# One small step per token group in a two-layer encoder kernel: three groups of narrow fp32 matmuls, placed side by side in TensorE's rows, are put into one place each and issued one kind after the other

## The chip, the cores and the metric

The kernel runs on one core of a Trainium2 chip. The metric is the device time in microseconds (us) of one execution. The time of a kernel is the median of several executions; the profiler also recorded one execution of the kernel before, and all rows of the trace come from that one.

## The reference

Two sequences (512 and 2048 tokens, 1024 wide) go through two layers. Each layer has one input projection, three groups of heads (RWKV-7 time mixing, latent attention, gMLP) and one output projection. The change touches only the preparation of the RWKV-7 branch (6 heads of 64 channels, 384 channels in all):

```python
kk = l2_normalize(heads(k * k_k))             # each head's 64 channels divided by their norm
def direction(d, lw, la, reverse):            # d = 0 forward, 1 backward
    w = jnp.exp(-DECAY_SCALE * jax.nn.sigmoid(decay_w0[d] + jnp.tanh(lw) @ decay_up[d]))
    a = jax.nn.sigmoid(iclr_a0[d] + la @ iclr_up[d])
    k_rep = k * (1 + (a - 1) * k_a)
    return wkv7_scan(heads(r), heads(w), kk, heads(a) * kk, heads(k_rep), heads(v), reverse)
```

`lw` and `la` have 64 columns for each direction, and `decay_up`, `iclr_up` are 64 x 384.

## The kernel before

All data are fp32, channels on the partitions. Each layer runs as a row of stages, with a barrier of all engines between two of them: `feature_projection`, `token_projection` (the one that is changed), `rwkv_scan`, `mla_attention`, `out_projection`.

`token_projection` does two things at once. TensorE computes the part of the input projection that is wanted token by token: 20 tiles of 128 tokens, three pieces each (512, 512 and 480 columns), 60 pieces (`project(n)`), each piece eight matmuls over the contraction; they use four of the eight PSUM banks, and ScalarE copies each piece out (`empty(n)`, L704). Between the pieces TensorE does the small products of the RWKV preparation for groups of 512 tokens, five groups (`g`), ten pieces beside each. The orders of TensorE, ScalarE, VectorE and SyncE are written out by hand, engine by engine. One fp32 matmul is two matmul instructions in the trace, each with its own weight load; the text calls such an instruction a pass.

The small products of a group, in TensorE's order, with `BA = 3` blocks `m` of 128 channels (two heads):

- `norm` (L851): the sums of squares of each head. Three matmuls accumulate into one bank. The constant matrix has `NR = 70` columns, so the six sums land three times, on partitions 0 to 5, 32 to 37 and 64 to 69. ScalarE takes the root of these 70 partitions (L760), VectorE bounds them from below and takes the reciprocal (L976, L978).
- `w` of direction 0 (L822, `lora`): three matmuls, contraction over 64 partitions.
- `bonus` (L863): three matmuls.
- piece n+1, then `inv` (L869): the six reciprocals are spread over the 128 channels of each block, by three matmuls with a contraction of 6. Block `m` reads partitions 32m to 32m+5, so the three stand in three different row groups of the array. VectorE multiplies `kk` with them (L988).
- `a` of direction 0 and `w` of direction 1 (L822): block by block in turn, a0, w0, a1, w1, a2, w2. Direction 0 reads partitions 0 to 63, direction 1 partitions 64 to 127. ScalarE takes the sigmoids in the same order (L710).
- pieces n+2, n+3, then `a` of direction 1 (L822, three matmuls), piece n+4, the block products (`blocks`, L839), pieces n+5 to n+9. The block products of direction 1 come after piece n+10 and before the next group's `norm`.

The small products share the other four banks in turn, in the order in which `uses.add` lists them; a product whose bank was used four places before waits until ScalarE or VectorE has emptied that one (`bank_free`). Around the change the places are: bonus 0, 1, 2, inv 0, 1, 2, then the six of `a` and `w`. VectorE's `direction(g, 0)` begins when the last `a` is through its sigmoid (L919), ScalarE's `blend` (L742) when L919 is done, and VectorE's `decay_sums(g, 1)` when the last `w` is.

Of the kernel before, what the change touches and what calls it, by code (L numbers as in the profile page):

```python
# [24 lines left out]
ACT = mybir.ActivationFunctionType  # L25
AX = mybir.AxisListType

P = 128
# [4 lines left out]
G = 512  # L33
# [4 lines left out]
HA, DH = 6, 64  # L38
BA = HA * DH // P
CH = 64  # L40
# [15 lines left out]
R_ADAB, R_QKW, R_LNW, R_LNB, R_ALL = np.cumsum([0, 3 * D, 2 * DQK, CW, CW]).tolist()  # L56

K_ID, K_BD, K_MA, K_KX, K_LV, K_RST, K_HS, K_HT, K_ALL = np.cumsum(
    [0, 128, 128, 512, 4 * CH, CH, 512, BA * (32 * (BA - 1) + HA), P]).tolist()


def slot_of(kind, parity):
# [431 lines left out]
def token_projection(l, wt, wt_in, nc, d, ps, kc, col, amod, eps, ident):  # L494
# [4 lines left out]
    HALF = (slice(0, CH), slice(CH, P))  # L499
    NP = 2 * BA * (G // SUB)  # L500
    PER = 10
    NR = 32 * (BA - 1) + HA
    pieces = [(n, c, min(c + 512, WT)) for n in range(NT) for c in range(0, WT, 512)]
    PT = len(pieces) // NT

# [3 lines left out]
    uses = Uses(4, 4)  # L509
# [5 lines left out]
    for g in range(NG):  # L515
        if g:
            add_blocks(g - 1, 1)
        for m in range(2):
            uses.add(("norm", g, m), "act")
        for m in range(BA):  # L520
            uses.add(("w", g, 0, m), "act")
        for m in range(BA):
            uses.add(("bonus", g, m), "dve")
        for m in range(BA):
            uses.add(("inv", g, m), "dve")
        for m in range(BA):
            uses.add(("a", g, 0, m), "act")
            uses.add(("w", g, 1, m), "act")
        for m in range(BA):
            uses.add(("a", g, 1, m), "act")  # L530
        add_blocks(g, 0)
    add_blocks(NG - 1, 1)

    with ExitStack() as ctx:
        def sb(name, shape):
            return ctx.enter_context(nc.sbuf_tensor(f"prep{l}_" + name, shape, F32))
# [5 lines left out]
        low = sb("low", [P, 2, G])  # L542
        ga = sb("ga", [P, BA, G])
        dup = sb("dup", [P, 2, BA * P])
        km = sb("km", [P, BA])
        norm = sb("norm", [NR, G])
        rkb = sb("rkb", [P, BA, P])
        kk = sb("kk", [P, BA, G])
        tmp = sb("tmp", [P, BA, G])
# [11 lines left out]
        with stage(nc, "up h_in0 h_in1 h_in2 rk_in0 rk_in1 val_in low_in ga_in z_filled z_out piece_sent0 piece_sent1 piece_sent2 "  # L561
# [136 lines left out]
            def _(a):  # L698
# [4 lines left out]
                    a.wait_ge(z_filled, n + 1)  # L703
                    a.activation(st[:, n % NB, 0:c1 - c0], ps[:, tiles.bank(pieces[n]), 0:c1 - c0], ACT.Copy).then_inc(z_out, 1)  # L704

                def sigmoid(kind, g, e, m):
                    out, c = {"w": (sg, C_W0), "a": (aa, C_A0)}[kind]
                    u = (kind, g, e, m)
                    a.wait_ge(filled, uses.ready(u))
                    a.activation(out[:, m, :], ps[:, uses.bank(u), :], ACT.Sigmoid, bias=col[:, c + e * BA + m:c + e * BA + m + 1]).then_inc(act_out, 1)  # L710

                def powers(g, e):
                    a.wait_ge(decayed, 2 * g + e + 1)
# [31 lines left out]
                for g in range(NG):  # L745
                    n = PER * g
                    a.wait_ge(rk_arrived[g % 2], 16 * (g // 2 + 1))
                    if g:
                        a.wait_ge(scaled_out, 2 * g)
                    for b in range(BA):  # L750
                        a.activation(kk[:, b, :], rk_in[g % 2][:, BA + b, :], ACT.Copy, scale=col[:, C_KK + b:C_KK + b + 1]).then_inc(keys, 1)
                    a.wait_ge(keys, BA * (g + 1))
                    a.activation(tmp[:, :, :], kk[:, :, :], ACT.Square).then_inc(squares, 1)
                    a.wait_ge(low_in, 16 * (g + 1))
                    a.activation(low[:, 0, :], low[:, 0, :], ACT.Tanh).then_inc(lora_in, 1)
                    empty(n)
                    if g:
                        blocks_out(g - 1, 1)
                    a.wait_ge(filled, uses.ready(("norm", g, 1)))
                    a.activation(norm[:, :], ps[0:NR, uses.bank(("norm", g, 0)), :], ACT.Sqrt).then_inc(act_out, 2)  # L760
                    for m in range(BA):
                        sigmoid("w", g, 0, m)
                    powers(g, 0)
                    a.wait_ge(filled, uses.ready(("bonus", g, BA - 1)))
                    for m in range(BA):
                        sigmoid("a", g, 0, m)
                        sigmoid("w", g, 1, m)
                    blend(g, 0)
                    empty(n + 1)
                    a.wait_ge(ga_in, 16 * (g + 1))  # L770
                    a.activation(ga[:, :, :], ga[:, :, :], ACT.Silu).then_inc(silu, 1)
                    empty(n + 2)
                    a.wait_ge(bonus_out, g + 1)
                    for m in range(BA):
                        last = a.activation(ga[:, m, :], ga[:, m, :], ACT.Copy, scale=col[:, C_GNW + m:C_GNW + m + 1])
                    last.then_inc(gated, 1)
                    empty(n + 3)
                    powers(g, 1)
                    a.wait_ge(scaled_out, 2 * g + 1)
                    for m in range(BA):  # L780
                        sigmoid("a", g, 1, m)
                    empty(n + 4)
                    blocks_out(g, 0)
                    empty(n + 5)
                    empty(n + 6)
                    if g:
                        turn(g - 1)
                    blend(g, 1)
                    empty(n + 7)
                    empty(n + 8)  # L790
                    empty(n + 9)
# [8 lines left out]
            def _(pe):  # L800
# [12 lines left out]
                def bank_free(u):  # L813
                    f = uses.former(u)
                    if f:
                        pe.wait_ge(act_out if f[0] == "act" else dve_out, f[1])
                    return ps[:, uses.bank(u), :]

                def lora(kind, g, e, m):
                    n = "wa".index(kind)  # L820
                    b = bank_free((kind, g, e, m))
                    pe.matmul(b, dup[DH * e:DH * e + DH, n, m * P:(m + 1) * P], low[DH * e:DH * e + DH, n, :], start=True, stop=True).then_inc(filled, 1)  # L822

                def blocks(g, e):
                    pe.wait_ge(scaled_out, 2 * g + e + 1)
# [16 lines left out]
                for g in range(NG):  # L842
                    n = PER * g
                    project(n)
                    if g:
                        blocks(g - 1, 1)
                    pe.wait_ge(squares, g + 1)
                    bank_free(("norm", g, 1))
                    b = bank_free(("norm", g, 0))
                    for m in range(BA):  # L850
                        last = pe.matmul(b[0:NR, :], kc[:, K_HS + m * NR:K_HS + (m + 1) * NR], tmp[:, m, :], start=(m == 0), stop=(m == BA - 1))  # L851
                    last.then_inc(filled, 2)
                    pe.wait_ge(lora_in, g + 1)
                    if g == 0:
                        pe.wait_ge(up, 32)
                    for m in range(BA):
                        lora("w", g, 0, m)
                    pe.wait_ge(rk, g + 1)
                    if g == 0:
                        pe.wait_ge(ready, 1 + BA)  # L860
                    for m in range(BA):
                        u = ("bonus", g, m)
                        pe.matmul(bank_free(u), rkb[:, m, :], aa[:, m, :], start=True, stop=True).then_inc(filled, 1)  # L863
                    project(n + 1)
                    pe.wait_ge(norms, g + 1)
                    for m in range(BA):
                        u = ("inv", g, m)
                        b = bank_free(u)
                        pe.matmul(b, kc[32 * m:32 * m + HA, K_HT:K_HT + P], norm[32 * m:32 * m + HA, :], start=True, stop=True).then_inc(filled, 1)  # L869
                    for m in range(BA):  # L870
                        lora("a", g, 0, m)
                        lora("w", g, 1, m)
                    project(n + 2)
                    project(n + 3)
                    for m in range(BA):
                        lora("a", g, 1, m)
                    project(n + 4)
                    blocks(g, 0)
                    project(n + 5)
                    project(n + 6)  # L880
                    project(n + 7)
                    project(n + 8)
                    project(n + 9)
# [1257 lines left out]
def shape_constants():  # L2141

    a, b = np.arange(P)[:, None], np.arange(P)[None, :]
    chunk = a // CH == b // CH
    k = np.zeros((P, K_ALL), np.float32)
# [13 lines left out]
    k[:, K_RST:K_RST + G] = np.arange(G) % CH != 0  # L2159
    for m in range(BA):  # L2160
        for h in range(HA):
            for n in range(BA):
                k[:, K_HS + m * (32 * (BA - 1) + HA) + 32 * n + h] = 2 * m + np.arange(P) // DH == h
            k[32 * m + h, K_HT:K_HT + P] = 2 * m + np.arange(P) // DH == h
    freqs = np.float32(10000.0) ** (-np.arange(16, dtype=np.float32) / np.float32(16))
    pos = np.concatenate([np.arange(T0), np.arange(T1)]).astype(np.float32)
    ang = (pos[:, None] * freqs[None, :]).astype(np.float32)
# [52 lines left out]
```

## Time and profile before

| | |
|---|---|
| median of 3 runs | 5484.08 us (5480.12 to 5485.88) |
| the profiled execution | 5480.12 us, span of its instructions 5478.1 us |
| busy: TensorE, weight loads, VectorE, ScalarE, GpSimd | 95%, 51%, 52%, 38%, 12% |
| mean granted TensorE clock | 0.983 |

A row of the timeline has the start and the length of a merged run of like instructions in us, the engine, the line of the kernel, the operation, what it writes and reads, the shapes, and the count; in brackets stands the idle time of the engine before it and what ended it. PE is TensorE's matmul side, PEld its weight loads, DVE VectorE, ACT ScalarE. A matmul's own length is modelled and overlaps the next one's, so the time that a run takes on TensorE is read from its start to the start of the next run.

### The profile page before, as it was taken

What the parts mean: (1) busy time and instruction counts of PE and PEld (TensorE: products, weight loads), DVE (VectorE), ACT (ScalarE), POOL (GpSimd) and SP (SyncE); (2) the same over time, 40 slices, a digit from 0 to 9 for tenths busy, and PEclk for the clock granted to TensorE, in tenths of its full rate; (3) what the DMA queues carried; (4) which work ended last, traced back from release to release, by engine and by line L of the source; (5) the groups of instructions that cost most, each with busy time, mean ns of one, the idle gap of its engine ahead of it and who ended that gap; (6) DMA issues with size and microseconds to landing.
All of it is one profiled execution on the core that took longest, in us unless ns stands there. A gap on an engine that the chain in (4) does not pass through costs nothing. (4 is left out here: it accounts for less than half of the span.)

```text
span 5478.1 us, 94771 instructions
## 1 busy us (share of the span) xinstructions
PE 5208.6 (95%) x38844; PEld 2808.7 (51%) x38844; DVE 2834.5 (52%) x4438; ACT 2068.8 (38%) x3470; POOL 641.6 (12%) x1110
## 2 busy tenths in 40 slices
PE   8999999899979999989989999998999799999899
PEld 3444444488854444444444444444788544444454
DVE  2221487555545555556522214875555555555565
ACT  1211556255544444421112115562455444444211
POOL 0000000044520000001100000000445200000011
PEclk9999999999999999999999999999999999999999
DMA  5311566565650111036343115664656501110353
GB/s 225 139 67 56 191 218 201 157 161 145 162 139 11 36 28 25 6 111 222 118 162 139 69 55 194 216 202 153 162 145 164 137 14 35 25 25 6 106 173 118
DMA packets 570089, 646.04 MB, mean 118 GB/s; under 512 B 228336, under 2 KB 455152, under 8 KB 559872
## 3 DMA queue, kind: packets, MB, share of 16 engines
q1 hardware_dynamic: 569072, 638.88, 37.3%
q8 instruction: 313, 5.13, 0.4%
q14 instruction: 112, 0.92, 0.1%
q10 hardware_dynamic: 592, 1.11, 0.1%
HBM read 372.74 MB, written 267.13 MB: 117 GB/s over the span
## 5 line engine op out<-in xcount | busy, mean ns | idle before, releaser
L490 PE MATMUL ps<-feat_hT,w_features 128*128 128x512 f32 x2240 | 972.5, 592 | 0.0
L810 PE MATMUL ps<-w_tokens,prep_hT 128*128 128x512 f32 (+1 forms) x1920 | 821.2, 587 | 23.1 <-DMA prep_hT<-s_ht 23.1
L1706 PE MATMUL ps<-att_K,att_Q 96*128 96x512 f32 x1632 | 744.3, 599 | 31.5 <-DMA att_K<-s_qkt 21.8
L490 PEld LDWEIGHTS ps<-feat_hT,w_features 128*128 128x128 f32 x2240 | 420.4, 190 | 505.9 <-issue 503.2
L1820 DVE TENSOR_REDUCE att_mx<-ps 128x1 f32<-128x1024 f32 x384 | 470.3, 1225 | 286.0 <-PE ps L1706 286.0
L810 PEld LDWEIGHTS ps<-w_tokens,prep_hT 128*128 128x128 f32 x1920 | 363.4, 191 | 469.5 <-issue 440.9
L1713 PEld LDWEIGHTS ps<-kc,att_pr 128*128 128x128 f32 x3264 | 362.8, 141 | 433.0 <-issue 319.1
L2101 PE MATMUL ps<-w_out,fin_yT 128*128 128x512 f32 x1280 | 569.0, 598 | 2.5 <-DVE fin_yT L2051 2.5
L1784 ACT ACTIVATE att_PT<-ps 128x512 f32<-128x512 f32 x384 | 228.1, 594 | 691.1 <-PE ps L1713 690.9
L1713 PE MATMUL ps<-kc,att_pr 128*128 128x128 f32 x3264 | 479.2, 279 | 5.3 <-DVE att_PT L1829 2.5
L1706 PEld LDWEIGHTS ps<-att_K,att_Q 96*128 96x128 f32 x1632 | 296.9, 192 | 334.0 <-issue 256.9
L1775 ACT ACTIVATE att_pr<-ps,att_nb 128x1024 f32<-128x1024 f32 x384 | 428.3, 1115 | 80.1 <-DVE att_nb L1822 80.0
L1829 DVE COPY att_PT<-ps 128x512 f32<-128x512 f32 x384 | 265.2, 691 | 322.0 <-PE ps L1713 322.0
L1729 PE MATMUL ps<-att_PT,att_V 128*64 128x512 f32 x1536 | 411.2, 617 | 0.3
L2101 PEld LDWEIGHTS ps<-w_out,fin_yT 128*128 128x128 f32 x1280 | 238.9, 192 | 274.8 <-issue 271.6
L380 ACT ACTIVATE feat_z<-ps 128x512 f32<-128x512 f32 x110 | 65.8, 598 | 603.8 <-PE ps L490 603.8
L1979 POOL TENSOR_SCALAR fin_rv<-fin_st 128x1 f32<-128x1 f32 x40 | 17.7, 442 | 2035.9 <-DVE fin_st L1997 2035.9
L419 DVE SCALAR_TENSOR_TENSOR feat_co<-feat_z,col,feat_co 128x512 f32<-128x512 f32 (+1 forms) x88 | 66.1, 751 | 300.1 <-ACT feat_co L352 300.1
L404 DVE TENSOR_SCALAR feat_hT<-ps,amod 128x512 f32<-128x512 f32 x80 | 63.8, 809 | 283.8 <-PE ps L477 283.6
L1421 DVE TENSOR_TENSOR scan_tok<-ps,scan_u 64x384 f32<-64x384 f32 x160 | 88.8, 555 | 218.1 <-PE ps L1542 190.2
L1252 POOL TENSOR_SCALAR scan_ss<-scan_ss 128x2 f32<-128x2 f32 x40 | 18.2, 455 | 1434.8 <-ACT scan_csq L1295 1434.8
L704 ACT ACTIVATE prep_st<-ps 128x512 f32<-128x512 f32 (+1 forms) x120 | 69.1, 583 | 268.1 <-PE ps L810 268.1
(226 smaller groups left out, 6735.8 us busy)
## 6 DMA issues: line engine op xcount, KB each, us to landing
s_sc<-prep_sc SPq DMA_DIRECT2D x20, 3072.0 KB, 9.0
scan_src<-s_sc SPq DMA_DIRECT2D x160, 384.0 KB, 4.9
s_qkt<-scan_qT SPq DMA_DIRECT2D x40, 576.0 KB, 4.2
fin_z<-s_zt SPq DMA_DIRECT2D x40, 576.0 KB, 5.1
s_zf<-feat_co SPq DMA_DIRECT2D x88, 256.0 KB, 2.6
s_ht<-feat_hT SPq DMA_DIRECT2D x10, 2048.0 KB, 7.9
prep_hT<-s_ht SPq DMA_DIRECT2D x40, 512.0 KB, 5.8
s_zt<-prep_st SPq DMA_DIRECT2D x80, 256.0 KB, 3.5
```

The costliest lines, as they stand in the source:

```text
L490: last = pe.matmul(b, wf[:, k, i * P:(i + 1) * P], hT[g % 2][:, k, :], start=(k == 0), stop=(k == KD - 1))
L704: a.activation(st[:, n % NB, 0:c1 - c0], ps[:, tiles.bank(pieces[n]), 0:c1 - c0], ACT.Copy).then_inc(z_out, 1)
L810: last = pe.matmul(ps[:, tiles.bank(pieces[n]), 0:c1 - c0], hT[j % NH][:, k, :], wt[:, k, c0:c1], start=(k == 0), stop=(k == KD - 1))
L1421: last = v.tensor_tensor(out_, pair(u, BA * CH)[HALF[p], :, :].rearrange("p o (m i) -> p o m i", m=BA), u0[HALF[p], s, :, :].rearrange("p ...
L1706: pe.matmul(ps[:, c, :], Q[:, t * P:(t + 1) * P], K[:, k0:k0 + G], start=True, stop=True).then_inc(scored, 1)
L1713: last = pe.transpose(ps[:, BANK_T + x % 2, k * P:(k + 1) * P], pr[:, n % 2, (TPG * x + k) * P:(TPG * x + k + 1) * P], ident)
L1729: last = pe.matmul(ps[DV * half:DV * half + DV, BANK_O, :], V[:, kb + (TPG if k else 0), 0:DV], PT[:, kb, :], start=(i == 0), stop=final_p ...
L1775: a.activation(pr[:, n % 2, 2 * half * G:2 * (half + 1) * G], ps[:, 2 * half:2 * half + 2, :].rearrange("p b n -> p (b n)"), ACT.Exp, bias ...
L1784: a.activation(evict_target(n, x), bank(BANK_T), ACT.Copy).then_inc(act_t, 1)
L1820: ch.link(v.tensor_reduce(mx[:, n % 2, half:half + 1], ps[:, 2 * half:2 * half + 2, :].rearrange("p b n -> p (b n)"), AX.X, ALU.max))
L1829: v.tensor_copy(evict_target(n, x), bank(BANK_T + 1)).then_inc(dve_t, 1)
L2101: last = pe.matmul(b, yT[n % TPG][:, k, :], wo[:, k, G * c:G * (c + 1)], start=(k == 0), stop=(k == KD - 1))
```

## The change

Three things are changed. The constant for the norms has 6 columns instead of 70, so that the six sums exist once, on partitions 0 to 5. The three `inv` matmuls all read these partitions, with three different 6 x 128 constants beside one another. And the six products of `a` (direction 0) and `w` (direction 1) are issued as a0, a1, a2, w0, w1, w2, with their banks and ScalarE's sigmoids in the same order. The constants' tile grows by 64 columns.

```diff
 K_ID, ..., K_HS, K_HT, K_ALL = np.cumsum(
-    [0, 128, 128, 512, 4 * CH, CH, 512, BA * (32 * (BA - 1) + HA), P]).tolist()
+    [0, 128, 128, 512, 4 * CH, CH, 512, BA * HA, BA * P]).tolist()
...
         for m in range(BA):
             uses.add(("a", g, 0, m), "act")
+        for m in range(BA):
             uses.add(("w", g, 1, m), "act")
...
-        norm = sb("norm", [NR, G])
+        norm = sb("norm", [HA, G])
...
-                    a.activation(norm[:, :], ps[0:NR, uses.bank(("norm", g, 0)), :], ACT.Sqrt).then_inc(act_out, 2)
+                    a.activation(norm[:, :], ps[0:HA, uses.bank(("norm", g, 0)), :], ACT.Sqrt).then_inc(act_out, 2)
...
-                    for m in range(BA):
-                        sigmoid("a", g, 0, m)
-                        sigmoid("w", g, 1, m)
+                    sigmoids("a", g, 0)
+                    sigmoids("w", g, 1)
...
-                        last = pe.matmul(b[0:NR, :], kc[:, K_HS + m * NR:K_HS + (m + 1) * NR], tmp[:, m, :], start=(m == 0), stop=(m == BA - 1))
+                        last = pe.matmul(b[0:HA, :], kc[:, K_HS + m * HA:K_HS + (m + 1) * HA], tmp[:, m, :], start=(m == 0), stop=(m == BA - 1))
...
                     for m in range(BA):
                         u = ("inv", g, m)
-                        b = bank_free(u)
-                        pe.matmul(b, kc[32 * m:32 * m + HA, K_HT:K_HT + P], norm[32 * m:32 * m + HA, :], start=True, stop=True).then_inc(filled, 1)
-                    for m in range(BA):
-                        lora("a", g, 0, m)
-                        lora("w", g, 1, m)
+                        pe.matmul(bank_free(u), kc[0:HA, K_HT + m * P:K_HT + (m + 1) * P], norm[:, :], start=True, stop=True).then_inc(filled, 1)
+                    lora("a", g, 0)
+                    lora("w", g, 1)
```

`lora` and `sigmoids` now hold the loop over the three blocks themselves; for `w` of direction 0 and `a` of direction 1 that is the order of before.

## Rows read from the trace of the kernel before

**Rows 1.** The page: span and the engines' busy time.

```profile
span 5478.1 us, 94771 instructions
PE 5208.6 (95%) x38844; PEld 2808.7 (51%) x38844; DVE 2834.5 (52%) x4438; ACT 2068.8 (38%) x3470; POOL 641.6 (12%) x1110
```

**Rows 2.** Windows, changed stage of layer 0: stretch, length, busy PE, PEld, DVE, ACT, POOL, clock.

```profile
552.00:1004.00 452.00, 444.44 (x1881) 195.56 (x1882) 319.97 (x462) 248.59 (x321) 0.00 (x0) 1.00 0.60 199
```

**Rows 3.** Timeline of the changed place in the first group.

```profile
576.90 1.13 PE L869 MATMUL ps<-prep_norm,kc 6*128 6x512 f32 x6
577.96 4.94 PE L822 MATMUL ps<-prep_low,prep_dup 64*128 64x512 f32 x12
578.05 1.89 DVE L988 TENSOR_TENSOR prep_kk<-ps,prep_kk 128x512 f32<-128x512 f32 x3 [3.04 <-PE ps L869]
578.80 0.29 PEld L822 LDWEIGHTS ps<-prep_low,prep_dup 64*128 64x128 f32 x2 [0.54 <-DVE prep_kk L988]
579.16 1.28 ACT L710 ACT_TABLE_LOAD   x1 [1.26 <-PE ps L822]
579.40 0.29 PEld L822 LDWEIGHTS ps<-prep_low,prep_dup 64*128 64x128 f32 x2 [0.30 <-DVE prep_kk L988]
...
580.46 0.69 ACT L710 ACTIVATE prep_aa<-ps,col 128x512 f32<-128x512 f32 x1
581.05 0.68 ACT L710 ACTIVATE prep_sg<-ps,col 128x512 f32<-128x512 f32 x1
581.20 0.29 PEld L822 LDWEIGHTS ps<-prep_low,prep_dup 64*128 64x128 f32 x2 [0.91 <-ACT prep_aa L710]
...
582.83 1.48 PE L810 MATMUL ps<-w_tokens,prep_hT 128*128 128x480 f32 x3
583.57 1.76 DVE L919 TENSOR_TENSOR prep_tmp<-prep_aa,prep_kk 128x1536 f32<-128x1536 f32 x1 [3.63 <-ACT prep_aa L710]
```

**Rows 4.** Timeline of PE at the same place in the last group of layer 1.

```profile
3674.20 1.13 PE L869 MATMUL ps<-prep_norm,kc 6*128 6x512 f32 x6
3675.27 4.94 PE L822 MATMUL ps<-prep_low,prep_dup 64*128 64x512 f32 x12
3680.14 1.12 PE L810 MATMUL ps<-w_tokens,prep_hT 128*128 128x512 f32 x2
```

**Rows 5.** Timeline of PE, then of its weight loads, at the products of one direction alone.

```profile
596.34 2.84 PE L822 MATMUL ps<-prep_low,prep_dup 64*128 64x512 f32 x6
599.11 1.12 PE L810 MATMUL ps<-w_tokens,prep_hT 128*128 128x512 f32 x2
596.34 0.29 PEld L822 LDWEIGHTS ps<-prep_low,prep_dup 64*128 64x128 f32 x2 [0.76 <-issue]
596.87 0.19 PEld L822 LDWEIGHTS ps<-prep_low,prep_dup 64*128 64x128 f32 x1 [0.24 <-issue]
597.30 0.19 PEld L822 LDWEIGHTS ps<-prep_low,prep_dup 64*128 64x128 f32 x1 [0.24 <-issue]
```

**Rows 6.** Timeline of PE before a two-column product in a later stage.

```profile
2692.42 1.02 PE L2101 MATMUL ps<-w_out,fin_yT 128*128 128x512 f32 x2
2693.37 0.60 PE L161 MATMUL ps<-fin_ada,sg 128*2 128x512 f32 x2
```

**Rows 7.** Timeline from the block products of one group to the next norms.

```profile
648.27 1.63 PE L839 MATMUL ps<-prep_sc 64*64 64x64 f32 x96
649.27 3.95 ACT L729 ACTIVATE prep_lst<-ps 32x384 f32<-32x384 f32 x8 [0.23 <-PE ps L839]
651.38 2.76 PE L851 MATMUL ps<-prep_tmp,kc 128*70 128x512 f32 x6 [1.48 <-ACT prep_lst L729]
```

**Rows 8.** What PE waited for at L851 in the whole span: us, times.

```profile
ACT prep_lst L729: 12.2, 8
```

**Rows 9.** Timeline of VectorE and PE before the second block products of a group.

```profile
731.26 1.83 DVE L898 TENSOR_TENSOR prep_sc<-prep_aa,prep_ip 128x768 f32<-128x768 f32 x2
737.90 1.63 PE L839 MATMUL ps<-prep_sc 64*64 64x64 f32 x96
```

More of the change, by code:

```diff
@@ L501, in token_projection @@
     PER = 10
-    NR = 32 * (BA - 1) + HA
     pieces = [(n, c, min(c + 512, WT)) for n in range(NT) for c in range(0, WT, 512)]
@@ L704, in empty, with sigmoids @@
                     a.activation(st[:, n % NB, 0:c1 - c0], ps[:, tiles.bank(pieces[n]), 0:c1 - c0], ACT.Copy).then_inc(z_out, 1)
-                def sigmoid(kind, g, e, m):
+                def sigmoids(kind, g, e):
                     out, c = {"w": (sg, C_W0), "a": (aa, C_A0)}[kind]
-                    u = (kind, g, e, m)
-                    a.wait_ge(filled, uses.ready(u))
-                    a.activation(out[:, m, :], ps[:, uses.bank(u), :], ACT.Sigmoid, bias=col[:, c + e * BA + m:c + e * BA + m + 1]).then_inc(act_out, 1)
+                    for m in range(BA):
+                        u = (kind, g, e, m)
+                        a.wait_ge(filled, uses.ready(u))
+                        a.activation(out[:, m, :], ps[:, uses.bank(u), :], ACT.Sigmoid, bias=col[:, c + e * BA + m:c + e * BA + m + 1]).then_inc(act_out, 1)
                 def powers(g, e):
@@ L759, in _ @@
                     a.wait_ge(filled, uses.ready(("norm", g, 1)))
-                    a.activation(norm[:, :], ps[0:NR, uses.bank(("norm", g, 0)), :], ACT.Sqrt).then_inc(act_out, 2)
-                    for m in range(BA):
-                        sigmoid("w", g, 0, m)
+                    a.activation(norm[:, :], ps[0:HA, uses.bank(("norm", g, 0)), :], ACT.Sqrt).then_inc(act_out, 2)
+                    sigmoids("w", g, 0)
                     powers(g, 0)
                     a.wait_ge(filled, uses.ready(("bonus", g, BA - 1)))
-                    for m in range(BA):
-                        sigmoid("a", g, 0, m)
-                        sigmoid("w", g, 1, m)
+                    sigmoids("a", g, 0)
+                    sigmoids("w", g, 1)
                     blend(g, 0)
@@ L779, in _ @@
                     a.wait_ge(scaled_out, 2 * g + 1)
-                    for m in range(BA):
-                        sigmoid("a", g, 1, m)
+                    sigmoids("a", g, 1)
                     empty(n + 4)
@@ L817, in bank_free, with lora @@
                     return ps[:, uses.bank(u), :]
-                def lora(kind, g, e, m):
+                def lora(kind, g, e):
                     n = "wa".index(kind)
-                    b = bank_free((kind, g, e, m))
-                    pe.matmul(b, dup[DH * e:DH * e + DH, n, m * P:(m + 1) * P], low[DH * e:DH * e + DH, n, :], start=True, stop=True).then_inc(filled, 1)
+                    for m in range(BA):
+                        b = bank_free((kind, g, e, m))
+                        pe.matmul(b, dup[DH * e:DH * e + DH, n, m * P:(m + 1) * P], low[DH * e:DH * e + DH, n, :], start=True, stop=True).then_inc(filled, 1)
                 def blocks(g, e):
@@ L855, in _ @@
                         pe.wait_ge(up, 32)
-                    for m in range(BA):
-                        lora("w", g, 0, m)
+                    lora("w", g, 0)
                     pe.wait_ge(rk, g + 1)
@@ L867, in _ @@
                         u = ("inv", g, m)
-                        b = bank_free(u)
-                        pe.matmul(b, kc[32 * m:32 * m + HA, K_HT:K_HT + P], norm[32 * m:32 * m + HA, :], start=True, stop=True).then_inc(filled, 1)
-                    for m in range(BA):
-                        lora("a", g, 0, m)
-                        lora("w", g, 1, m)
+                        pe.matmul(bank_free(u), kc[0:HA, K_HT + m * P:K_HT + (m + 1) * P], norm[:, :], start=True, stop=True).then_inc(filled, 1)
+                    lora("a", g, 0)
+                    lora("w", g, 1)
                     project(n + 2)
                     project(n + 3)
-                    for m in range(BA):
-                        lora("a", g, 1, m)
+                    lora("a", g, 1)
                     project(n + 4)
@@ L2161, in shape_constants @@
         for h in range(HA):
-            for n in range(BA):
-                k[:, K_HS + m * (32 * (BA - 1) + HA) + 32 * n + h] = 2 * m + np.arange(P) // DH == h
-            k[32 * m + h, K_HT:K_HT + P] = 2 * m + np.arange(P) // DH == h
+            k[:, K_HS + m * HA + h] = 2 * m + np.arange(P) // DH == h
+            k[h, K_HT + m * P:K_HT + (m + 1) * P] = 2 * m + np.arange(P) // DH == h
     freqs = np.float32(10000.0) ** (-np.arange(16, dtype=np.float32) / np.float32(16))
```

## The prediction

> **What bounds the kernel now.** I read the page first: TensorE is busy for 95% of the span, every other engine for about half or less [rows 1]. The windows of the changed stage say the same of the place itself: of 452 us TensorE is busy for 444, at the full granted clock (1.00, the level of 2.4 GHz), VectorE for 320, ScalarE for 249 [rows 2]. So the stage is as long as TensorE's list of passes, and the question is what the change does to that list, then whether a wait of TensorE swallows or adds something. Then I read the timeline at the place. The three `inv` matmuls, six passes, take from 576.90 to 577.96, 1.06 us, and the six products of `a` and `w`, twelve passes, from 577.96 to 582.83, 4.87 us: 5.93 together [rows 3]. In the last group of layer 1 it is 1.07 and 4.87 again, 5.94 [rows 4]. The ten places (five groups, two layers) agree to a hundredth of a us, so I work out one and multiply by ten.
>
> **The price of one pass.** Where three matmuls of the same shape as `a` and `w` stand in one row group (direction 1 alone), the first pass starts at 596.34, the next at 596.87, then 597.30: 0.53, and from then on 0.43 a pass [rows 5]. The 0.10 over is the weight load that nothing covers on the first pass. From the last pass to the next piece it is 0.52 (596.34 + 0.53 + 4 x 0.43 = 598.59, next start 599.11). Six serial passes so take 2.77 us, entry and exit included [rows 5]. The six `inv` passes of before take 1.06, that is two passes' time and the exit [rows 3]: the three row groups do run at once. That is the whole gain of the old layout there.
>
> **Part 1: `inv` in one row group.** Six passes one behind the other cost what the six of rows 5 cost, 2.77 instead of 1.06: +1.71 us a group. The trace has no run of matmuls with a contraction of 6 in one row group, so the bounds are: 2.77 as in rows 5, and, if every pass pays 0.53 as a first one does, 5 x 0.53 + 0.52 = 3.17, +0.40. I take 2.77, because only the number of partitions differs and the time of a pass is that of its 512 columns in both. Below 2.77 I see nothing, since the partitions are the same ones.
>
> **Part 2: a0, a1, a2, w0, w1, w2.** The old order alternates between partitions 0 to 63 and 64 to 127, so passes can overlap; w0 starts at 578.80 and a1 at 579.40, 0.60 later where two serial passes take 0.96 [rows 3]. But it hardly uses that, because it runs into its banks: w0 waits for VectorE to empty the bank of inv 0 (first load at 578.80), a1 and w1 for the next two, a2 for ScalarE's first sigmoid (581.20, idle 0.91) and w2 for the second [rows 3]. It gets 4.87, where twelve serial passes with entry and exit are 0.53 + 10 x 0.43 + 0.52 = 5.35. Now the new order, in us from the first `inv` pass:
> - The `a` passes begin at 2.77: a0 at 2.77 and 3.30, a1 at 3.73 and 4.16, a2 at 4.59 and 5.02. Their banks: a0 follows bonus 2, a1 follows inv 0, a2 inv 1, w0 inv 2. VectorE takes 0.69 for each and began 1.15 after the first pass (578.05), that is 0.62 after that block's second pass [rows 3]; now it begins at 1.15, 2.01 and 2.87 and the banks are free, 0.74 later, at 1.9, 2.8 and 3.6. None of them is waited for any more.
> - w0 reads the other half, so its first pass starts with a2's last one, at 5.02, the second at 5.55, through at 5.98.
> - w1 needs the bank of a0. ScalarE's table load began 0.67 after a0's second pass began (578.49 to 579.16), the sigmoid 1.30 later, it took 0.69, and TensorE went on 0.05 after [rows 3]. Now: 3.30 + 0.67 + 1.30 + 0.69 + 0.05 = 6.01. w1 starts at 6.01 with its load uncovered, 6.53, and w2 (its bank, a1's, is free at 6.6) at 6.96 and 7.39; the next piece starts 0.52 later, at 7.91.
> So the `a` and `w` part takes 7.91 - 2.77 = 5.14 instead of 4.87: +0.27. If w0 did not overlap a2's last pass, it would be the serial 5.35, +0.48; if neither overlap nor waits cost anything more than they do here, it cannot be under 5.35 - 0.43 = 4.92, +0.05.
>
> **Part 3: the norms with 6 columns.** The number of passes stays six. ScalarE's root and VectorE's bound and reciprocal have 512 elements on each partition as before, so their lengths stay. What may change is the entry: a product with few columns behind a full one starts 0.95 after the last but one full pass began (2692.42 to 2693.37), where two passes are 0.86 [rows 6], so such a change costs 0.09. In eight of the ten groups the norms stand behind the block products and a wait of about 1.5 for ScalarE [rows 7, 8], which covers it, and the weight load there, no longer 70 columns wide, may be some hundredths shorter. That leaves 0.09 in the first group of each layer, 0.2 us in all, and perhaps as much back: I take nothing, with bounds of -0.5 and +2.0 (a full 0.20 of entry and uncovered load in all ten groups). The 64 more columns of constants are 32 KB at the start, behind the first transposes' wait, which other work ends; nothing.
>
> **What the other engines do with it.** The last `a` is through its sigmoid 0.57 later than now (a2's sigmoid is the third in ScalarE's row instead of the fifth, but the row starts 1.71 later), so L919 starts about 0.6 later and everything behind it on VectorE too, while TensorE's next piece starts 1.98 later. VectorE's last operation before the block products ended at 733.09, and they began at 737.90 [rows 9]: this slack of 4.8 grows. ScalarE's last `w` sigmoid comes some 1.7 later, but `blend` waits for L919 anyway. `low` is read no longer than before as seen from TensorE's later products, and SyncE's queue has nothing new. So nothing gets late, and nothing that TensorE waits for gets earlier in a way that it would feel.
>
> **Sum.** 1.71 + 0.27 = 1.98 us a group, ten groups: +19.8 us. The profiled execution took 5480.12 us (2.0 of it outside the span of 5478.1), so it would be 5499.9. The median of the runs is 5484.08, 3.96 above that execution; on it I get 5503.9.
>
> **Rivals.**
> - *TensorE's wait swallows it.* In eight groups TensorE waits before the norms for ScalarE's copies L729, 12.2 us in all [rows 8]. Were those copies held by something that does not move with TensorE, the wait would shrink by the delay: 19.8 - 12.2 = +7.6, 5491.7, within 0.2%. It decides from 8.8 us swallowed (1.1 of the 1.5 in each). Against it: L729 starts 1.0 after the block products began and was itself waiting for them (idle 0.23, released by PE) [rows 7], so the wait moves along whole. This is the one way that ends at "not slower".
> - *`inv` pays its loads.* With 0.53 for each pass, 0.40 more a group: +23.8, 5507.9.
> - *Every pass in one row group pays its load.* Five more in `inv` and ten or so in `a` and `w`, 15 x 0.10 = 1.5 a group: +35, 5519. Rows 5 speak against it: the loads of passes three and four follow at 0.43 in the same row group. By the Trainium skill (TensorE: Matmul & The Clock Gate, in "Part 3: Packing small matmuls — row/col tiling") a weight load overlaps a running matmul only where the row group differs; by that the sum would be this one, by the row it is mine. The trace disagrees with the rule, at 0.43 a pass.
> - *No overlap of w0 with a2:* +0.21 a group, 5506.0.
>
> **How the numbers follow.** The forecast has 0.78, no overlap 0.07, `inv` paying its loads 0.06, every pass paying 0.02, the swallowed delay 0.04, and 0.03 is left for something faster that I can't name from the rows. Runs of one kernel spread by 5.8 us here, so 0.2% (11 us) is what can be told from no change. The range runs from 5496 (the forecast less its bounds of 2.2 for part 2 and 0.5 for part 3, and the spread) to 5511 (`inv` with its loads, and the spread). Slower by over 0.2% then has 0.93, within it 0.04, faster 0.03.
>
> **What would show it.** In the profile after: L869's six passes from start to the next run's start 2.77 (3.17 if loads are paid); the `a` and `w` run 5.14, with one wait of TensorE for the first sigmoid and none for VectorE's L988; L919 starting 7.24 after the first `inv` pass instead of 6.67; the wait before the norms still 1.5; busy time of TensorE higher by about 20 us, and the slack before the second block products above 6. The prediction is wrong if the `inv` passes in one row group still take about 1.1, or if the ten groups lengthen by another amount than the place itself does.

## The result, and the profile of the changed kernel

The changed kernel takes 5519.53 us (median of four runs, 5514.96 to 5524.57), the kernel before 5484.26. The ratio is 1.0065, 95% interval 1.0048 to 1.0083: 0.65% slower. I had forecast slower, by 19.8 us; it is 35.3, and 5519.5 lies above the range that I gave (5496 to 5511). The profiled execution is not one of the four and was longer than all of them: 5531.59 us, span 5529.7.

The page of the kernel after, against [rows 1]: TensorE 45.3 us more of busy time and 18.5 more of weight loads, the other engines as before, the number of instructions the same.

```profile
span 5529.7 us, 94771 instructions
PE 5253.9 (95%) x38844; PEld 2827.2 (51%) x38844; DVE 2836.4 (51%) x4438; ACT 2069.1 (37%) x3470; POOL 641.7 (12%) x1110
```

The timeline of PE at the changed place, in the first and third group of layer 0 and in the last of layer 1, where [rows 3, 4] have 5.93 and 5.94 us from the first `inv` pass to the next piece:

```profile
577.85 2.84 PE L866 MATMUL ps<-prep_norm,kc 6*128 6x512 f32 x6
580.61 5.78 PE L821 MATMUL ps<-prep_low,prep_dup 64*128 64x512 f32 x12
586.33 1.88 PE L808 MATMUL ps<-w_tokens,prep_hT 128*128 128x480 f32 x4
...
762.58 2.84 PE L866 MATMUL ps<-prep_norm,kc 6*128 6x512 f32 x6
765.35 7.87 PE L821 MATMUL ps<-prep_low,prep_dup 64*128 64x512 f32 x12
773.15 1.22 PE L808 MATMUL ps<-w_tokens,prep_hT 128*128 128x512 f32 x1
...
3717.67 2.84 PE L866 MATMUL ps<-prep_norm,kc 6*128 6x512 f32 x6
3720.44 5.78 PE L821 MATMUL ps<-prep_low,prep_dup 64*128 64x512 f32 x12
3726.15 1.12 PE L808 MATMUL ps<-w_tokens,prep_hT 128*128 128x512 f32 x2
```

The `inv` passes take what I said, 2.77 (577.85 to 580.61, 762.58 to 765.35; 2.96 and 2.99 in two of the ten groups). The passes of `a` and `w` do not: 5.72, 7.80, 5.71 instead of 5.14. And the ten places are no longer alike, which is the first hint that it is not a matter of the instruction list. The windows of two of these `inv` and `a`/`w` stretches show what it is (stretch, length, busy PE, PEld, DVE, ACT, POOL, then the granted clock):

```profile
577.84:580.61 2.77, 2.77 (x7) 1.03 (x6) 1.38 (x2) 1.00 (x1) 0.00 (x0) 1.00 0.00 0
580.61:586.32 5.71, 5.71 (x13) 2.56 (x12) 1.04 (x2) 3.68 (x5) 0.00 (x0) 0.70 0.00 0
762.58:765.35 2.77, 2.77 (x7) 1.03 (x7) 1.38 (x2) 1.00 (x1) 0.00 (x0) 1.00 0.00 0
765.35:773.15 7.80, 7.80 (x14) 3.06 (x13) 2.28 (x2) 4.39 (x6) 0.00 (x0) 0.51 0.01 2
```

TensorE is busy without a gap through the `inv` passes, at a granted clock of 1.00, and in the stretch behind them it runs at 0.70 and 0.51: part or nearly all of it at the lower of its two levels, 1.2 GHz instead of 2.4. In the two groups with 2.96 and 2.99 the clock falls before the last `inv` pass is through (0.93 and 0.92 over those passes). The same windows at all ten places have a clock of 0.50 to 0.70 and a mean length of 6.76 us where I had 5.14:

```profile
sum 67.62, PE 67.62 PEld 28.44 DVE 16.86 ACT 40.81 POOL 0.00; mean PE 6.76 PEld 2.84 DVE 1.69 ACT 4.08 POOL 0.00
```

The whole stage of layer 0 was at 1.00 before [rows 2]; now, over the same work:

```profile
553.00:1026.00 473.00, 466.12 (x1881) 204.06 (x1882) 320.88 (x462) 249.58 (x321) 0.00 (x0) 0.96 0.59 195
```

From TensorE's first piece to the last group's second block products the stage of layer 0 takes 476.6 us (553.27 to 1029.89) where it took 455.3 (552.48 to 1007.80), and that of layer 1 475.8 where it took 455.0: +42.1 in both, 19.8 of passes and 22.3 more. Of the 22.3 some 16.6 lie in the ten places themselves (5.7 at the least, 7.9 at the most for `a` and `w`), the rest in the pieces behind. The other 9.5 us by which the profiled execution's span grew lie outside the changed stage; 7.1 of them between its last block products and the first attention passes, where `rwkv_scan` stands (599.6 and 600.8 us in the two layers, where it was 596.8 and 596.4).

### The profile page after: what moved, and what is told of

Same layout as the page of the kernel before. It is cut to its first block and busy times, and to the rows that moved or that the text cites. A ratio compares the mean times of both kernels' runs of the same rounds, so it can differ in the third digit from the quotient of the medians.

```text
span 5529.7 us, 94771 instructions
## 1 busy us (share of the span) xinstructions
PE 5253.9 (95%) x38844; PEld 2827.2 (51%) x38844; DVE 2836.4 (51%) x4438; ACT 2069.1 (37%) x3470; POOL 641.7 (12%) x1110
## 5 line engine op out<-in xcount | busy, mean ns | idle before, releaser
L808 PEld LDWEIGHTS ps<-w_tokens,prep_hT 128*128 128x128 f32 x1920 | 365.8, 192 | 475.8 <-issue 450.2
```

Of the source, the lines that this page charges most:

```text
L808: last = pe.matmul(ps[:, tiles.bank(pieces[n]), 0:c1 - c0], hT[j % NH][:, k, :], wt[:, k, c0:c1], start=(k == 0), stop=(k == KD - 1))
```

## Experiments

To compare the runs I read one more view of each: the granted clock over the 12 us from the first `inv` pass, at the ten places. "Falls" below is the number of places where it is under 1.00. The kernel before has 0, the changed one 10. The count comes from one profiled execution of each kernel. Each time is a median, with the ratio to runs of the kernel before on the same chip and its 95% interval; the ratio can differ by up to 0.06% from the quotient of the two medians, and where a text below gives microseconds, they are the difference of the medians.

| run | what differs | us (before) | ratio (interval) | falls |
|---|---|---|---|---|
| e1_inv_only | alternating a, w; serial inv | 5505.32 (5478.42) | 1.0054 (1.0040 to 1.0067) | 9 |
| e2_order_only | grouped a, w; inv as before | 5487.73 (5478.42) | 1.0014 (1.0005 to 1.0024) | 1 |
| e3_inv_full_rows | changed, inv over 128 partitions | 5494.73 (5478.42) | 1.0034 (1.0022 to 1.0047) | 0 |
| e4_piece_between | changed, a piece behind inv | 5580.24 (5478.42) | 1.0187 (1.0173 to 1.0201) | 10 |
| e5_inv_32_rows | changed, inv over 32 partitions | 5509.95 (5482.71) | 1.0052 (1.0033 to 1.0071) | 6 |
| e6_inv_64_rows | changed, inv over 64 partitions | 5495.97 (5482.71) | 1.0024 (1.0012 to 1.0035) | 0 |
| e7_norm_70_columns | changed, norms 70 columns | 5520.50 (5482.71) | 1.0067 (1.0050 to 1.0084) | 10 |
| e8_three_times_side_by_side | before, inv three times over | 5517.64 (5482.71) | 1.0065 (1.0050 to 1.0080) | 10 |
| e9_two_row_groups | changed, inv in two row groups | 5509.80 (5482.30) | 1.0056 (1.0043 to 1.0070) | 7 |
| e10_tables_early | before, ScalarE tables early | 5469.17 (5482.30) | 0.9972 (0.9963 to 0.9982) | 0 |
| e11_changed_again | the changed kernel | 5518.75 (5482.30) | 1.0068 (1.0054 to 1.0082) | 10 |

### One part at a time: e1_inv_only and e2_order_only

```diff
# e1_inv_only, against the kernel after
-                    lora("a", g, 0)
-                    lora("w", g, 1)
+                    for m in range(BA):
+                        lora("a", g, 0, [m])
+                        lora("w", g, 1, [m])
...
# e2_order_only, against the kernel before
                     for m in range(BA):
                         lora("a", g, 0, m)
+                    for m in range(BA):
                         lora("w", g, 1, m)
```

In both the banks and the sigmoids follow the same order.

> The changed kernel with the six products of a and w put back in the alternating order a0, w0, a1, w1, a2, w2; the norms with 6 columns and the three inv products in one row group stay. Theory 1 (the six serial inv passes, which use 6 rows, make the granted clock of TensorE fall; the grouped order of a and w only adds its +0.27 a group): the clock shows stretches at half in most of the ten groups as in the changed kernel, and the time is +17 us of passes plus 10 to 30 us of lost clock over the kernel before, 5511 to 5530. Rival 2 (the grouped order, 5.1 us of passes in one half of the rows behind the inv passes, is needed for the fall): no half-clock stretches in the groups, 5501.

> The kernel before with one part of the change: a0, a1, a2, w0, w1, w2 in banks, on TensorE and on ScalarE; the inv products stay in three row groups and the norms keep 70 columns. Theory 1: about +0.3 us a group, 5487, no half-clock stretch in the groups. Rival 2: half-clock stretches appear in the groups, 5497 or more.

The serial `inv` passes alone bring the falls (9 of 10) and 26.9 of the microseconds. The one place without a fall shows the bare price in TensorE's timeline:

```profile
3703.43 2.84 PE L866 MATMUL ps<-prep_norm,kc 6*128 6x512 f32 x6
3706.20 1.99 PE L821 MATMUL ps<-prep_low,prep_dup 64*128 64x512 f32 x8
3709.43 1.70 PE L821 MATMUL ps<-prep_low,prep_dup 64*128 64x512 f32 x4 [1.25 <-ACT prep_aa L710]
3711.06 1.12 PE L808 MATMUL ps<-w_tokens,prep_hT 128*128 128x512 f32 x2
```

That is 7.64 us, 1.70 more than before, all of it `inv`. The 26.9 is the low end of the 27 to 47 expected over the kernel before. The grouped order alone costs 9.3 us by the medians (interval 3 to 13); its place takes 6.21 us in nine of ten groups (before 5.94, so +0.27, as summed), 2.7 us in all. The tenth had a fall behind `inv` passes of only 1.06 us:

```profile
3405.27 1.13 PE L871 MATMUL ps<-prep_norm,kc 6*128 6x512 f32 x6
3406.34 7.46 PE L824 MATMUL ps<-prep_low,prep_dup 64*128 64x512 f32 x12
```

So the order adds a little of each, and serial `inv` passes are not the only thing that a fall can stand behind. How many falls there are seems to change from run to run: of the eleven runs of e2 the shortest, 5474.05 us, has a mean clock of 0.984 and the longest, 5496.92, one of 0.980. But the grouped order is not needed for the falls (e1 has nine without it), and rival 2 is out.

### Are six-row passes the cause: e3_inv_full_rows, e6_inv_64_rows, e5_inv_32_rows

```diff
-        norm = sb("norm", [HA, G])
+        norm = sb("norm", [P, G])
...
-                        pe.matmul(bank_free(u), kc[0:HA, K_HT + m * P:K_HT + (m + 1) * P], norm[:, :], start=True, stop=True).then_inc(filled, 1)
+                        pe.matmul(bank_free(u), kc[:, K_HT + m * P:K_HT + (m + 1) * P], norm[:, :], start=True, stop=True).then_inc(filled, 1)
...
+                v.memset(norm[:, :], 0.0).then_inc(ready, 1)
```

(e5 and e6: 32 and 64 in place of P. The added rows hold zeros on both sides, so the sums stay.)

> The changed kernel, but each inv product contracts over all 128 partitions: the tile of reciprocals has 128 partitions with zeros in 122 of them, and the constants are zero there too. The number of serial passes and their columns stay. Theory 1 in the form that the few rows in use matter: the clock stays at full level in the groups, and the time is the +1.98 a group of my sum or a little less (no change of row group before inv), 5500 to 5504. If only that the passes are serial, or that their products are mostly nothing, matters: as the changed kernel, 5515 to 5530.

> As e3_inv_full_rows, but with a contraction over 64 partitions (58 of them zero). The products of a and w, and those of w and a alone elsewhere in the group, use 64 rows and the clock does not fall at them in the kernel before. If rows decide: few falls or none, and +17 to +25. If falls come as in the changed kernel, zeros or the run of 7.9 us without a pass over all rows matter.

> As e3_inv_full_rows, but the inv products contract over 32 partitions (26 of them zero) instead of 128. If the clock goes by the number of rows of the array that the serial passes use, and 32 are still few: falls at most of the ten places, as in the changed kernel, +27 to +41 over the kernel before. If 6 rows were the special case: no falls, +16 to +20.

The passes are as many and as serial as in the changed kernel, the numbers that they multiply are zeros where they were nothing, and the falls are gone at 128 and 64 partitions, while 32 partitions had 6. The times follow: +16.3, +13.3, +27.2; the first two are 3 to 4 us less than expected. The timeline of e3 has the place at full clock:

```profile
580.78 2.74 PE L866 MATMUL ps<-prep_norm,kc 128*128 128x512 f32 x6
583.45 2.84 PE L821 MATMUL ps<-prep_low,prep_dup 64*128 64x512 f32 x8
586.69 1.98 PE L821 MATMUL ps<-prep_low,prep_dup 64*128 64x512 f32 x4 [0.40 <-ACT prep_aa L711]
588.60 1.88 PE L808 MATMUL ps<-w_tokens,prep_hT 128*128 128x480 f32 x4
```

`inv` 2.67, `a` and `w` 5.15, together 7.82; my sum had 2.77 and 5.14. The 0.10 that `inv` is short of tells what the entry is paid for: here `inv` contracts over as many partitions as the piece before it, and its first load (580.36) runs beside that piece's last pass. In e6 it is the first `a` that follows passes with as many partitions as its own, 64, and there `a` and `w` take 5.04. So where TensorE has no wait before a run, the 0.10 of entry goes with a change in the number of rows. In e5 a place without a fall shows the sum itself, 763.02 to 770.93, 7.91:

```profile
763.02 2.84 PE L866 MATMUL ps<-prep_norm,kc 32*128 32x512 f32 x6
765.79 2.84 PE L821 MATMUL ps<-prep_low,prep_dup 64*128 64x512 f32 x8
769.02 1.98 PE L821 MATMUL ps<-prep_low,prep_dup 64*128 64x512 f32 x4 [0.40 <-ACT prep_aa L711]
770.93 1.55 PE L808 MATMUL ps<-w_tokens,prep_hT 128*128 128x512 f32 x3
```

### One row group, or few rows for long: e8_three_times_side_by_side and e9_two_row_groups

```diff
# e8_three_times_side_by_side, against the kernel before
-                        pe.matmul(b, kc[32 * m:32 * m + HA, K_HT:K_HT + P], norm[32 * m:32 * m + HA, :], start=True, stop=True).then_inc(filled, 1)
+                    for r in range(3):
+                        for m in range(BA):
+                            b = ps[:, uses.bank(("inv", g, m)), :]
+                            last = pe.matmul(b, kc[32 * m:32 * m + HA, K_HT:K_HT + P], norm[32 * m:32 * m + HA, :], start=True, stop=True)
+                            if r == 2:
+                                last.then_inc(filled, 1)
...
# e9_two_row_groups, against the kernel after: AT = (0, 32, 0), the sums on partitions 0 to 5 and 32 to 37
+                        pe.matmul(bank_free(u), kc[AT[m]:AT[m] + HA, K_HT + m * P:K_HT + (m + 1) * P], norm[AT[m]:AT[m] + HA, :], start=True, stop=True).then_inc(filled, 1)
```

> The kernel before with its three inv products issued three times over (the first two results are overwritten by the same values), in their three row groups: 18 passes that take about 1.06 + 2 x 0.86 = 2.8 us, as long as the six serial ones of the changed kernel, with three row groups at work instead of one. VectorE's first product comes 1.7 later, all three banks at once, so a and w run 4.87 as before: +1.7 a group, +17. If the rows at work decide: no falls, +17. If it is the length of a stretch of products with a contraction of 6: falls at most places, +27 or more.

> The changed kernel with the sums on partitions 0 to 5 and 32 to 37: inv 0 and inv 2 read the first copy, inv 1 the second, so that two of the three products overlap and the inv passes take about 1.06 + 0.86 = 1.9 us instead of 2.77. If the length of the stretch of 6-row passes makes the clock fall, 1.9 us lies between the 1.06 that never had a fall and the 2.8 that had one at nearly every place: falls at some of the ten places, +12 to +25. If any serial 6-row product does it: falls at most places, +25 or more. If only a stretch as long as 2.8 does: none, +12.

e8 is the surprise: three row groups at work, falls at all ten places. The windows of its `inv` stretch (18 passes in 2.78 us), of the `a` and `w` stretch behind it and of the 12 us from its start:

```profile
578.93:581.71 2.78, 2.78 (x19) 1.10 (x19) 0.00 (x0) 1.01 (x1) 0.00 (x0) 1.00 0.00 0
581.71:586.94 5.23, 5.23 (x15) 2.69 (x12) 1.89 (x3) 3.65 (x6) 0.00 (x0) 0.67 0.00 0
578.93:590.93 12.00, 12.00 (x41) 5.80 (x41) 5.14 (x6) 7.33 (x11) 0.00 (x0) 0.86 0.01 1
```

So being placed in one row group is not what lowers the clock; three times six rows side by side for 2.8 us do it as well, and for 1.06 us, as in the kernel before, they don't. In e9 the `inv` passes take 1.91 us, in between, and 7 of 10 places fall.

The time of e8 can't be taken for the price of its falls, though it is nearly that of the changed kernel. All ten places have 0.86 over their 12 us, 0.14 x 12 = 1.7 us of clock each, and the fall lies within the `a` and `w` stretch (0.33 x 5.23 = 1.7). But that stretch takes 5.2 to 5.3 us where it took 4.87, so most of the 1.7 costs nothing there; TensorE had idle loads of 0.91 and 0.28 us in this stretch before, waiting for ScalarE, which may be what hides it. The changed stage grew by 10.7 and 11.2 us in the two layers (467.7 and 467.9 us from the first piece to the end of the last block products, where it was 457.0 and 456.7): 2.2 a group, 1.72 of it passes. The profiled execution's span grew by 38.9, and the other 17.0 lie outside the changed stage, most of them where `rwkv_scan` of layer 0 stands. The kernel before first, then e8:

```profile
1009.43:1606.22 596.79, 532.46 (x11701) 432.00 (x11700) 315.59 (x488) 276.34 (x477) 242.95 (x342) 0.97 0.54 143
1022.12:1630.46 608.34, 541.12 (x11701) 438.90 (x11701) 315.31 (x488) 276.51 (x477) 242.69 (x342) 0.96 0.53 140
```

Why the clock is lower there too, in a stage that no edit touched, stays open.

### Apart from a and w: e4_piece_between

```diff
+                    project(n + 2)
                     lora("a", g, 0)
                     lora("w", g, 1)
-                    project(n + 2)
                     project(n + 3)
```

> The changed kernel with piece n+2 (sixteen full passes, some 7 us) moved between the inv products and those of a and w. If the six inv passes alone make the clock fall: half-clock stretches stay, now in the piece, 5512 or more. If it takes the inv passes and the grouped passes of half the rows in one row (8 us without a full pass): no half-clock stretches in the groups, and the sum of before holds, 5504 to 5506.

Falls at all ten places, now in the piece: the `inv` passes suffice, with full passes behind them too. But the time, +101.8, is no measure of that, as the edit makes `a` late on ScalarE and VectorE. What e4 waits for at the block products (L838), over the whole span:

```profile
PE ps L838 <- ACT prep_aa L711: 39.8, 12, 4.1
```

These waits were none before. They stand at the first block products of each group, 3.7 to 4.1 us each (and two of 0.2), not at the second ones of [rows 9], whose slack holds. In the first group:

```profile
604.69 7.13 PE L808 MATMUL ps<-w_tokens,prep_hT 128*128 128x512 f32 x16
614.68 1.84 ACT L711 ACTIVATE prep_aa<-ps,col 128x512 f32<-128x512 f32 x3
615.51 2.72 PE L838 MATMUL ps<-prep_sc 64*64 64x64 f32 x96 [3.69 <-ACT prep_aa L711]
```

The sigmoids of `a` of direction 1 must empty a bank first. Before, they began at 604.10 and the block products came at 606.17 without a wait; the edit leaves one piece where two stood between the six products of the place and `a` of direction 1. I had not priced it.

### The norms' columns, and the changed kernel again: e7_norm_70_columns and e11_changed_again

```diff
# e7_norm_70_columns, against the kernel after
-    last = pe.matmul(b[0:HA, :], kc[:, K_HS + m * HA:K_HS + (m + 1) * HA], tmp[:, m, :], ...)
+    last = pe.matmul(b[0:NR, :], kc[:, K_HS + m * NR:K_HS + (m + 1) * NR], tmp[:, m, :], ...)
```

> The changed kernel with the norms' constant left at 70 columns, so that the sums stand three times; the three inv products still all read partitions 0 to 5. If the 6-column norms have no part in the falls: as the changed kernel, falls at most places, +30 to +41. If they have: fewer falls, near +20.

> The changed kernel once more, beside the other two on one chip. If the clock's falls are a property of the kernel: half-clock stretches at nearly all of the ten places again, of 3 to 10 us each in another mix, and +27 to +45. If the first profile was an odd one: near +20 with few falls.

With 70 columns the time and the falls are those of the changed kernel: the 6-column norms have no part in it. The changed kernel again has a fall at every place, with window clocks from 0.62 to 0.86 (first profile 0.61 to 0.86) in another mix, and +36.5.

### A version that beats both: e10_tables_early

The place had shown (ahead of the prediction) that a2 waits for ScalarE's first sigmoid, and that its table is loaded only once TensorE's product is there. One activation of one column, whose result nothing reads, brings the load forward; a second one does so for the norms' root.

```diff
+                    a.activation(early[:, 0:1], eps[:, 3:4], ACT.Sqrt)
                     a.wait_ge(filled, uses.ready(("norm", g, 1)))
...
                     powers(g, 0)
+                    a.activation(early[:, 1:2], eps[:, 3:4], ACT.Sigmoid)
                     a.wait_ge(filled, uses.ready(("bonus", g, BA - 1)))
```

> The kernel before with two more ScalarE activations of one column a group, whose results nothing reads: a Sqrt before ScalarE waits for the norms and a Sigmoid before it waits for the bonus products. Each makes ScalarE load its table (1.28 us) while it would wait anyway. The first sigmoid of a then begins about 1.2 us earlier, and TensorE's waits for ScalarE's banks at a2 and w2 (0.91 and 0.28 of idle weight loads) shrink by some 0.6 in sum; the norms' root comes 1.0 earlier, some 0.3 to 0.5 less of waiting at w2 of direction 0 and at the bonus products. Expected -0.9 a group, -9, 5470 to 5475 where the kernel before has 5480. If those waits are not ScalarE's table but something else: no change.

```profile
579.14 1.13 PE L872 MATMUL ps<-prep_norm,kc 6*128 6x512 f32 x6
579.36 1.28 ACT L766 ACT_TABLE_LOAD   x1
580.21 4.02 PE L825 MATMUL ps<-prep_low,prep_dup 64*128 64x512 f32 x12
580.66 0.20 ACT L766 ACTIVATE prep_early<-eps 128x1 f32<-128x1 f32 x1
581.43 0.69 ACT L711 ACTIVATE prep_aa<-ps,col 128x512 f32<-128x512 f32 x1 [0.57 <-PE ps L825]
584.16 1.07 PE L813 MATMUL ps<-w_tokens,prep_hT 128*128 128x480 f32 x2
```

The load now runs from 579.36, beside the `inv` passes; the first sigmoid starts 1.22 us after the `a` run begins instead of 2.50, and the run takes 3.95 us instead of 4.87. The place is 5.02 instead of 5.94. From the second group's norms to its piece it is 8.14 (652.70 to 660.84) instead of 8.61. Some 1.4 us a group, ten groups: 14, and 13.1 measured where I had expected 9: 0.28% faster than the kernel before (interval 0.18 to 0.37).

## Why the prediction was wrong

- **The step that failed is the first one:** that the place runs "at the full granted clock (1.00, the level of 2.4 GHz)", read from the stage before the change, and then every pass of the new list priced at 0.43. The list was right, the price was not: behind the serial `inv` passes the granted clock falls to the lower level, at 10 of 10 places in both profiles of the changed kernel. The missing term is 22 us in the profiled stage; by the medians it is 35.3 - 19.8 = 15.5, some 1.5 us a group. None of my rivals named the clock.
- **Shown:** the stretch of few-row `inv` passes, 1.9 to 2.8 us long, brings the falls: e1 and e4 have it without the grouped order behind it and fall at 9 and 10 of 10 places; e3 and e6 have the same number of serial passes over more rows and don't; e8 falls with three row groups at once. The rows added in e3 and e6 hold only zeros and the clock stays up, so it is the number of rows that the passes use that counts, and not the numbers multiplied. Not explained by it is the one fall of e2, behind 1.06 us of `inv`.
- **`inv` in one row group, +1.71:** right. 2.77 where the clock held, and past the first pass no load is paid: the weight loads in the changed kernel are 0.43 apart (578.38, 578.81, 579.24, 579.67 in the first group). The rival "every pass pays its load" gave 5519, the measured number, for a reason that these starts refute; a hit of the total alone proves nothing.
- **`a` and `w`, +0.27:** the sum was right (5.15 in e3, 5.15 in e2), the picture inside not. I let w0 start with a2's last pass and w1 wait 0.03. In e3 the first eight passes, w0's two among them, run from 583.45 for 2.84 us, in which six serial ones just fit (2.84 in [rows 5]), and TensorE then idles 0.40 until ScalarE frees a0's bank. The loads show when w0 ran:

```profile
583.45 0.29 PEld L821 LDWEIGHTS ps<-prep_low,prep_dup 64*128 64x128 f32 x2 [0.76 <-DVE prep_kk L985]
583.99 0.19 PEld L821 LDWEIGHTS ps<-prep_low,prep_dup 64*128 64x128 f32 x1 [0.24 <-issue]
584.42 0.62 PEld L821 LDWEIGHTS ps<-prep_low,prep_dup 64*128 64x128 f32 x4 [0.24 <-issue]
585.27 0.19 PEld L821 LDWEIGHTS ps<-prep_low,prep_dup 64*128 64x128 f32 x1 [0.24 <-issue]
```

  Four loads stand within 0.62 us, where one row group takes one in 0.43; two of the four are w0's. Its passes begin at 584.42 and 584.95, beside a1's at 584.41 and 584.84 and ahead of a2's at 585.27 and 585.70. So w0 was done before a2 was; w1 starts when ScalarE lets it in either way (6.00 after the first `inv` pass in e5, forecast 6.01), and that set the end.
- **The norms, nothing:** right within noise (e7 against e11: 5520.50 and 5518.75).
- **The swallowed wait:** the changed kernel has it as before, 1.5 at the norms; the trace shows TensorE waiting there for the same copies, so it moved along.
- **The ten places alike:** they were before and at full clock in e3; with falls of differing length each is another. That the spread of the runs comes from this is likely and not shown. What made the span longer outside the changed stage (9.5 us in the first profile, 17.0 in e8) I have not isolated. Why falls last 3 us at one place and 10 at another is open too.

## What to carry to other kernels

A stretch of matmuls on few partitions is not only poorly used time; stretches of 1.9 to 2.8 us were followed here, at most of the places, by 3 to 10 us at the lower clock, although TensorE was busy throughout. Before serializing small products, or repeating them, compare the granted clock in windows of single stretches, not of a stage; and if partitions can be padded with zeros (64 here), the same pass count cost 13 us instead of 35 to 38. When a product waits for ScalarE's bank behind a table load, a one-column activation issued ahead of the wait is worth trying.

## What was unexpected of the hardware

- The granted clock fell by the number of partitions contracted over, in serial `inv` passes of 2.7 us: 6 partitions 10 of 10 places (9 in e1), 32 partitions 6, 64 and 128 none. By the Trainium skill (TensorE: Matmul & The Clock Gate, "Part 1: The HAM clock gate (the "warmup" mystery)") a monitor of TensorE's busy-ness sets one of two levels. The two levels agree with the rows; busy-ness as the profile counts it does not explain them: TensorE was busy 2.77 of 2.77 us ahead of the fall.
- Two row groups do not keep to one order: in e3, w0's passes, issued behind a2's, begin at 584.42 and 584.95 and a2's at 585.27 and 585.70, and the eight passes take the time of six. By the Trainium skill (same page, "Part 3: Packing small matmuls — row/col tiling") matmuls start and end strictly in program order; the trace disagrees where the row groups differ.
